# Attention keys and queries projected with the weights stationary and rotated block by block, in one fused attention and mLSTM layer

## The reference

```python
h = rms_norm(x, pre_norm_g[l])
proj = jnp.einsum('bsd,dc->bsc', h, w_in[l])
aq, ak, av, az, mq, mk, mv, mo, mz, mi, mf = split_columns(proj)
ya = moba_attention(partial_rope(att_heads(aq), pos), partial_rope(att_heads(ak), pos), att_heads(av))

def partial_rope(x, pos):            # ROT_DIM = 16 of the 64 columns of a head
    x1 = x[..., :half]
    x2 = x[..., half:ROT_DIM]
    return jnp.concatenate([x1 * cos - x2 * sin, x2 * cos + x1 * sin, x[..., ROT_DIM:]], axis=-1)
```

## Time and profile before

| what | value |
|---|---|
| runs | 323.36 us median (323.27 to 323.56) |
| the profiled execution | 323.28 us, its span 321.5 us |
| PE busy | 313.4 us, 97%, 1626 matmuls |
| DVE busy | 223.3 us, 69%, 527 instructions |
| ACT busy | 167.9 us, 52% |
| POOL busy | 88.2 us, 27% |
| granted TensorE clock | 0.998 |

### The profile page before, as it was taken

One profiled execution on the slowest core, in us unless ns is written; L12 is line 12 of the kernel. 1 busy time (PEld: TensorE's weight loads), 2 busy tenths in 40 slices (PEclk: granted clock), 3 DMA queues, 4 the chain that ended last, 5 costly groups with the idle time before them and its releaser, 6 DMA issues.

```text
span 321.5 us, 5021 instructions
## 1 busy us (share of the span) xinstructions
PE 313.4 (97%) x1626; PEld 260.5 (81%) x1626; DVE 223.3 (69%) x527; ACT 167.9 (52%) x336; POOL 88.2 (27%) x112
## 2 busy tenths in 40 slices
PE   7999999999999999999999999999999999999993
PEld 5887887878888888888888888778888888888882
DVE  2444999758998479976897557775577676865534
ACT  3538852697345434664257442374655976443201
POOL 8001003206350222002220015592621895001000
PEclk9999999999999999999999999999999999999999
DMA  7931553943735491144723332210120264310111
GB/s 234 294 84 50 152 154 92 167 133 93 129 76 143 133 166 39 31 135 139 137 65 98 100 86 80 65 66 34 44 88 2 100 207 153 134 65 2 65 65 65
DMA packets 27016, 33.50 MB, mean 104 GB/s; under 512 B 3768, under 2 KB 15328, under 8 KB 26992
## 3 DMA queue, kind: packets, MB, share of 16 engines
q1 hardware_dynamic: 25712, 30.38, 31.7%
q0 software_dynamic: 1120, 2.68, 6.3%
q10 hardware_dynamic: 160, 0.14, 0.1%
HBM read 31.06 MB, written 2.13 MB: 103 GB/s over the span
## 4 chain that ended last, share of the span: by engine, by line
PE 82%; DVE 9%; issue 5%; ACT 2%; DVEq 0%; POOLq 0%; POOL 0%; ACTq 0%
PE bank L1437 20%; PE bank L1439 20%; PE bank L1438 20%; PE bank L1484 4%; PE bank L1777 3%; PE bank L1721 3%; PE bank L1742 3%; DVE w_lo L980 2%; PE bank L1563 2%; PE bank L1465 1%; DVE farena L1091 1%; PE bank L1671 1%; ACT w_hi L731 1%; DVE rarena L987 1%; PE bank L1732 1%
## 5 line engine op out<-in xcount | busy, mean ns | idle before, releaser
L1437 PE MATMUL bank<-w_hi,xT_hi 128*128 128x512 f32 (+1 forms) x244 | 98.3, 403 | 0.0
L1439 PE MATMUL bank<-w_hi,xT_lo 128*128 128x512 f32 (+1 forms) x244 | 94.9, 389 | 0.0
L1438 PE MATMUL bank<-w_lo,xT_hi 128*128 128x512 f32 (+1 forms) x244 | 94.3, 387 | 0.0
L731 ACT ACTIVATE w_hi<-w_raw 128x512 fp32r<-128x512 f32 x72 | 43.9, 625 | 55.2 <-PE bank L1439 53.1
L1439 PEld LDWEIGHTS bank<-w_hi,xT_lo 128*128 128x128 f32 x244 | 45.8, 188 | 9.8
L1437 PEld LDWEIGHTS bank<-w_hi,xT_hi 128*128 128x128 f32 x244 | 45.9, 188 | 8.0 <-issue 0.4
L1438 PEld LDWEIGHTS bank<-w_lo,xT_hi 128*128 128x128 f32 x244 | 46.0, 189 | 7.6
L980 DVE TENSOR_TENSOR w_lo<-w_raw,w_hi 128x512 fp32r<-128x512 f32 x64 | 45.0, 718 | 4.8 <-ACT w_hi L731 4.5
L908 ACT ACTIVATE rarena<-bank 128x512 fp32r<-128x512 f32 (+3 forms) x32 | 13.9, 436 | 22.5 <-PE bank L1777 22.5
L1437 PE MATMUL bank<-xT_hi,w_hi 128*128 128x512 f32 x64 | 25.6, 400 | 0.0
L1439 PE MATMUL bank<-xT_hi,w_lo 128*128 128x512 f32 x64 | 25.1, 392 | 0.0
(11 more groups left out here) (206 smaller groups left out, 595.8 us busy)
## 6 DMA issues: line engine op xcount, KB each, us to landing
w_raw<-in_w_in SPq DMA_DIRECT2D x72, 256.0 KB, 2.8
w_raw<-in_w_out SPq DMA_DIRECT2D x16, 256.0 KB, 2.6
gy<-in_x SPq DMA_DIRECT2D x4, 512.0 KB, 5.4
out_y<-gy SPq DMA_DIRECT2D x7, 256.0 KB, 2.0
farena<-in_x SPq DMA_DIRECT2D x4, 256.0 KB, 4.7
farena<-in_x SPq DMA_DIRECT2D x2, 512.0 KB, 6.6
farena<-g_rows POOLq DMA_DIRECT2D x4, 256.0 KB, 4.0
farena<-g_rows POOLq DMA_DIRECT2D x4, 192.0 KB, 5.8
```

The source lines that it names most:

```text
L731: a.activation(w_hi[:, n % RING, :], w_raw[:, n % RAW, :], ACT.Copy).then_inc(w_hi_done, 1)
L1437: pe.matmul(o, hi, m_hi, start=start, stop=False)
L1438: pe.matmul(o, hi, m_lo, start=False, stop=False)
L1439: return pe.matmul(o, lo, m_hi, start=False, stop=stop)
```

## The change

- Keys and queries are projected with the weights stationary (`by_block`): the block m of 128 columns (two heads) lies on the partitions, the tokens lie along the row, and nothing has to be turned. `turn_k`, `turn_q`, `k_copy`, `q_copy` and the old `rope` go.
- The rotation works on whole blocks: `plain` = block x cosine table and `crossed` = block with its rows exchanged by a shuffle of 32 partitions (both on DVE, from PSUM, `kq_rows`), then on POOL (`kq_sum`) `crossed` x sine table and the sum of both. The high and low parts are then taken from SBUF (`k_high`, `k_low`, `q_high`, `q_low`).
- The tables are full: 128 partitions by 512 tokens, with 1 and 0 where nothing rotates. Four DMAs of POOL load the short table in the first microseconds, PE turns it once (`rope_rows`, in bank 6), ACT copies four parts of it (`rope_part`), and POOL multiplies both tables by the norm of x (`tables`). The sine table lies in `gains` until the queries are done, so the second gain row is loaded later.
- The groups' order becomes az, ak, aq, av. Values are copied by ACT to `stage` and split from there.
- Gate rows: the input gate's bias goes to ACT, the negation of the maxima to ACT, the last difference (`rows[4]`) to POOL. `gate_cols` uses bank 7; `emt` is taken in loop 18, behind both silus of head 0.
- On POOL the sums stand between the decay rows, the square roots and the masks of heads 2 and 3.

The diff, cut to its core:

```diff
-for _h, _c in enumerate((AZ, AK, AV, AQ)):
+for _h, _c in enumerate((AZ, AK, AQ, AV)):
...
-                if n == S_AV + 4:
-                    sp.wait_ge(az_gained, NT)
+                if n == S_MO:
+                    sp.wait_ge(kq_ready, 2 * NT)
                     sp.dma_start(gains[:], mlstm_g.to_broadcast([P, AW])).then_inc(gain_in, 16)
...
+            for q in range(4):
+                g.dma_start(rope_cols[:, :, q, 0:ROT],
+                            rope[:, ROT * (q % 2):ROT * (q % 2 + 1)].rearrange("(t p) c -> p t c", p=P)).then_inc(rope_in, 16)
...
+            g.wait_ge(gmax_done, 1)
+            g.tensor_tensor(rows[4], rows[1], rows[2], ALU.subtract).then_inc(grows_done, 1)
...
-            for h in range(1, MH):
-                decay_rows(h)
-                head_rsqrt(2 * h - 2)
-                decay_mask(h)
-                head_rsqrt(2 * h - 1)
+            def tables():
+                g.wait_ge(rope_rows_done, 4)
+                g.wait_ge(rbc_done, 1)
+                g.tensor_tensor(cos_t, cos_raw, rbc[:], ALU.mult).then_inc(tables_done, 1)
+                g.tensor_tensor(sin_t, sin_raw, rbc[:], ALU.mult).then_inc(tables_done, 1)
+            def kq_sum(w, m):
+                n = NT * w + m
+                g.wait_ge(tables_done, 2)
+                g.wait_ge(kq_crossed, n + 1)
+                g.tensor_tensor(crossed[w][:, m, :], crossed[w][:, m, :], sin_t, ALU.mult).then_inc(kq_scaled, 1)
+                g.wait_ge(kq_scaled, n + 1)
+                g.wait_ge(kq_plain, n + 1)
+                g.tensor_tensor(plain[w][:, m, :], plain[w][:, m, :], crossed[w][:, m, :], ALU.add).then_inc(kq_ready, 1)
+            decay_rows(1)
+            head_rsqrt(0)
+            decay_mask(1)
+            head_rsqrt(1)
+            tables()
+            for w in range(2):
+                kq_sum(w, 0)
+                kq_sum(w, 1)
+                decay_rows(w + 2)
+                head_rsqrt(2 * w + 2)
+                kq_sum(w, 2)
+                head_rsqrt(2 * w + 3)
+                kq_sum(w, 3)
+                decay_mask(w + 2)
...
+            a.activation(rows[6], gate_rows[0:16, :], ACT.Identity, bias=bcol[:, 0:1]).then_inc(igate_done, 1)
...
-                if b == S_QK + 7:
+                if b == ST_AT[0]:
                     a.wait_ge(aT_done, 1)
...
+            def k_high(m):
+                a.wait_ge(kq_ready, m + 1)
+                a.activation(kT_hi[:, m, :], plain[0][:, m, :], ACT.Copy).then_inc(kt_hi, 1)
...
+            def kq_rows(w, m):
+                projected(v, ("ak", "aq")[w], m)
+                v.wait_ge(tables_done, 2)
+                if w:
+                    v.wait_ge(kq_ready, m + 1)
+                    v.wait_ge(kt_lo, m + 1)
+                v.tensor_tensor(plain[w][:, m, :], bank[m][:], cos_t, ALU.mult).then_inc(kq_plain, 1)
+                v.stream_shuffle(crossed[w][:, m, :], bank[m][:],
+                                 [i // ROT * ROT + (i + HALF) % ROT for i in range(32)]).then_inc(kq_crossed, 1)
...
+                    for m in (2 * c, 2 * c + 1):
+                        if b == S_AQ - 3 + c:
+                            kq_rows(0, m)
+                        if b == S_AV - 3 + c:
+                            kq_rows(1, m)
+                        if b == S_MZ + 3 + c:
+                            v_low(m)
...
+            def by_block(n, k, free):
+                low_done(pe, n)
+                for m in range(4):
+                    if k == 0:
+                        free(m)
+                    mm = product(bank[m][:], *w_part(n, slice(m * P, (m + 1) * P)), xT_hi[:, k, :], xT_lo[:, k, :],
+                                 k == 0, k == NK - 1)
```

More of the change, by code:

```diff
@@ L113 @@
 EVENTS = {}
-PRIORITY = ("mz", "mz_late", "z", "slot", "z_part", "part", "part_q", "q_T", "q_out", "ya_half", "ya", "ya_sq", "ya_ms",
+PRIORITY = ("mz", "mz_late", "z", "slot", "z_part", "part", "part_q", "q_out", "ya_half", "ya", "ya_sq", "ya_ms",
             "ya_gate", "y_sq", "y", "y_q_sq", "y_q", "y_fin", "y_end", "cut", "turn")
@@ L312, in build @@
         bcol = pcol[0:16, R_BIAS:R_END]
-        keys = queries = stage
+        plain, crossed = (stage, gate), (gate, stage)
+        cos_t, sin_t = f_part(F_COS, SEQ), gains[:]
+        cos_raw, sin_raw = stage[:, 3, :], stage[:, 2, :]
+        rope_cols = silu_az[:, 3, :].rearrange("p (t q d) -> p t q d", t=NT, q=4)
         post = stage[:, 0:2].rearrange("p a c -> p (a c)")
@@ L426, in build @@
         ym_gated = sem("ym_gated")
-        k_raw = sem("k_raw")
-        k_roped = sem("k_roped")
-        kt_ps = sem("kt_ps")
+        rope_clear = sem("rope_clear")
+        rope_ps = sem("rope_ps")
+        rope_set = sem("rope_set")
+        rope_rows_done = sem("rope_rows_done")
+        tables_done = sem("tables_done")
+        kq_plain = sem("kq_plain")
+        kq_crossed = sem("kq_crossed")
+        kq_scaled = sem("kq_scaled")
+        kq_ready = sem("kq_ready")
+        v_raw = sem("v_raw")
         kt_hi = sem("kt_hi")
@@ L783, in decays, with rope_part @@
                     .then_inc(decay_done, 1)
+            def rope_part(q):
+                a.wait_ge(rope_ps, 1)
+                a.wait_ge(rope_set, 2)
+                to = 2 * ROT * (q // 2 * 2)
+                a.activation((cos_raw, sin_raw)[q % 2][to:to + 2 * ROT, :], bank[6][2 * ROT * q:2 * ROT * (q + 1), :],
+                             ACT.Copy).then_inc(rope_rows_done, 1)
             def conv_silu(n):
@@ L832, in _ @@
                 if b == S_MZ + 1:
-                    for i in range(NT):
-                        q_copy(i)
+                    for t in range(NT):
+                        v_copy(t)
                 cut(b + AHEAD)
@@ L1559, in head_values @@
                     pe.wait_ge(num_done, NT * h + t - 1)
+                else:
+                    pe.wait_ge(emt_done, 1)
                 o = bank[7 - t % 2]
@@ L1579, in _ @@
             rx_rows()
+            rope_rows()
             mv_slot(NK - 1)
@@ L1598, in qk_slot @@
                 mm.then_inc(w_used, 1)
-            def turn_k(t):
-                pe.wait_ge(k_roped, t + 1)
-                if t < 2:
-                    pe.wait_ge(u_done, 5 + t)
-                else:
-                    pe.wait_ge(kt_lo, t - 1)
-                for k in range(4):
-                    mm = pe.transpose(bank[4 + t % 2][:, k * P:(k + 1) * P], keys[:, t, k * P:(k + 1) * P], ident[:])
-                mm.then_inc(kt_ps, 1)
-            def turn_q(i):
-                pe.wait_ge(q_roped, i + 1)
-                if i < 2:
-                    pe.wait_ge(u_done, 7 + i)
-                else:
-                    pe.wait_ge(qt_lo, i - 1)
-                for k in range(4):
-                    mm = pe.transpose(bank[4 + i % 2][:, k * P:(k + 1) * P], queries[:, i, k * P:(k + 1) * P], ident[:])
-                mm.then_inc(qt_ps, 1)
+            def by_block(n, k, free):
[5 more added lines that the diff above has]
+                                 k == 0, k == NK - 1)
+                    if k == NK - 1 and m < 3:
+                        mm.then_inc(proj_ps, 1)
+                mm.then_inc(w_used, 1)
             def mz_slot(b):
-                by_slot(b, b - S_MZ, NK, x_part, lambda t: pe.wait_ge(q_raw, t + 1))
+                by_slot(b, b - S_MZ, NK, x_part, lambda t: pe.wait_ge(v_raw, t + 1))
             for b in range(S_QK, LAST_SLOT):
@@ L1718, in pair_scores @@
                     for q, half in enumerate(rows_of):
-                        lhs = qT[half, 2 * i + (step == 2), cols]
+                        lhs = (q_lo if step == 2 else q_hi)[half, h // 2, t * P:(t + 1) * P]
                         keys_of = kT_lo if step == 1 else kT_hi
```

205 lines of the change are left out of this document (79 added, 126 removed).

## The result

| what | before | after |
|---|---|---|
| runs | 323.35 us median (323.27 to 323.85) | 330.47 us median (330.25 to 333.15) |
| ratio | | 1.0242 (1.0207 to 1.0277) |
| profiled execution, span | 323.28, 321.5 us | 330.62, 328.9 us |

What follows compares the result with a forecast made beforehand. PE, busy for 97% of the span, was taken as the bound, with DVE's small reserves deciding. -3.5 + 0.44 - 0.89 + 0.95 + 3.4 + 0.75 + 3.2 = +4.35 us on 323.28 gave 327.6 us, range 320.3 to 331.0.

Steps and rivals of the forecast that it cites:

- Transposes, -3.5 + 0.44: On PE, 32 transposes of roped keys and queries go, -3.5 us; one group for the table rows comes, +0.44.
- The gate steps, -0.89: PE's stall at 70.25 to 71.37 goes: three gate operations leave DVE, emt moves behind both silus; 0.89 us gained.
- The tables, +0.95: Loops 28 to 30: POOL's two table products hold DVE, weighted ends near 104.05, PE waits 0.95 us.
- Keys, +3.4, and queries, +3.2: Loops 33 to 40 and 45 to 52: new DVE work and POOL's holds delay qk_low; PE waits 3.4 and 3.2 us.
- the same terms: The keys' chain of DVE steps reused for the queries, from 150.16 to 179.1, wanted at 175.89.
- weighted(2,0), +0.75: One step after the keys' wait: ACT's late silu puts DVE's weighted at 144.55, PE ready at 143.8; 0.75 us.
- the first steps of attention: Value copies go through stage and v_low stands where ropes of the same length stood; no cost counted.
- What the profile would show: Waits of 3.4, 3.2 at qk_low, 0.95 at weighted; convolution additions over 0.9 us, low cut over 0.8, POOL some 110.
- Rival 1: POOL's work finds gaps, DVE loses nothing, only PE's work counts: -3.95, 319.3 us; chance 0.18.
- the locks: POOL's operations hold about 1.25 us each; DVE operations with two SBUF inputs wait, those with a PSUM input do not.
- Rival 2: POOL's hold on DVE costs half of what was counted, 4.15 of 8.3 us of stalls: 323.5 us; chance 0.13.
- Rival 3: The shuffle takes 1.2 us, 2.2 us more in each stretch: 332.0 us; chance 0.05, including late table rows.

Runs made afterwards that it cites:

- 2: The changed kernel without DVE's eight shuffles (rotation left out, POOL's 16 operations keep their length): 327.31 us.
- 4: The changed kernel with the rotation's products and sums on DVE in place of POOL, k_high and k_low two loops later: 322.32 us, ratio 0.9965.
- the first of 5: The changed kernel with POOL's two table products put ahead of the decay rows of head 1: 331.85 us.
- 10: The kernel before, with only DVE's copy of the gate columns one loop earlier (14 instead of 15): 322.75 us, ratio 0.9982.
- 9: Changed kernel with sums on DVE, tables behind weighted(1,1), values one loop earlier, v_copy awaiting its own block, emt put back between ACT's two silus: 320.51 us.
- 11: The kernel before with extra DVE subtractions ahead of qk_low(5) and qk_low(7): six and six 333.31 us, three and nine 331.21 us.

## Why the prediction was right and wrong

- **Transposes, -3.5 + 0.44.** Right: the page has 28 PE instructions less, no turning in slots 37 to 40 and 59 to 62, and the group for the table rows costs 0.43 us (33.84 to 34.27). In this trace everything from the first slots on is another 0.5 us late:
```profile
33.84 0.60 PE L1546 MATMUL bank<-ident,rx 128*128 128x128 f32 x4
34.27 0.60 PE L1554 MATMUL bank<-ident,silu_az 128*128 128x128 f32 x4
```

and the `rx` group before:

```profile
33.30 0.60 PE L1527 MATMUL bank<-ident,rx 128*128 128x128 f32 x4
```

That is no cost of the change: the `rx` group starts at 33.26 to 33.28 in the traces of 2, 4 and the first of 5, which load the tables in the same way, and at 33.56 in that of 10, which loads none.
- **The gate steps, -0.89.** The size was right (PE's gap at 70 is gone), the reason wrong in half. emt's new place is not needed (9); the earlier copy of the gate columns and the shorter gate steps are what counts (10).
- **The tables, +0.95.** Measured 1.07. The way was not quite the one told: `hsc` waits 1.25 us and the norm's two steps, with one SBUF input each, take 1.53 where I let two cuts be held:

```profile
99.31 1.31 POOL L661 TENSOR_TENSOR farena<-stage,rbc 128x512 f32<-128x512 f32 x1
99.38 1.25 DVE L1201 TENSOR_TENSOR hsc<-vr,iden 128x2 f32<-128x2 f32 x1
...
100.55 1.31 POOL L662 TENSOR_TENSOR gains<-stage,rbc 128x512 f32<-128x512 f32 x1
...
100.67 1.53 DVE L1203 TENSOR_SCALAR gy<-num,mva,hsc 128x128 f32<-128x128 f32 x2
...
104.15 0.41 PE L1456 MATMUL bank<-rarena 128*128 128x384 f32 x1 [0.91 <-DVE farena L1154]
```

- **Keys, +3.4, and queries, +3.2.** Measured 3.39 and 3.41. For the queries "the same terms" were added 0.3 us too low (from 169.8 they give 175.7 and 179.4, so 3.5). That the sums hit is in part luck, since they rest on errors that cancel: the convolution's first step was taken to run freely beside POOL and was held for 1.0 us (1.50 against 0.55), while its additions lost 0.9 and 1.1 us and not 1.9 and 2.35. And the terms do not simply add (2).
- **weighted(2,0), +0.75.** Not seen in the kernel after, since PE itself was slow there; it comes out, as 0.77, where the clock stays up (2).
- **What was missing, first:** the clock. I priced a wait of PE at its length. Behind the first one another 1.5 us went (1.85 to 2.0 by the differences between runs), and in two of six runs, by their mean clock, probably a second time. This is the step that failed: a wait put on PE was taken to go on the time at its own length, with no term for what comes after it.
- **What was missing, second:** the first steps of attention. "Value copies go from PSUM through stage ... v_low stands where ropes of the same length stood" let them cost nothing: a term set to zero, the second step that failed. Two `v_low` took 2.38 and 2.06 us beside POOL's cuts, and q_low and the norm were held as well:

```profile
213.00 2.55 POOL L644 TENSOR_TENSOR w_lo<-w_raw,w_hi 128x512 fp32r<-128x512 f32 x2
213.08 1.24 DVE L1201 TENSOR_TENSOR hsc<-vr,iden 128x2 f32<-128x2 f32 x1
214.35 1.53 DVE L1203 TENSOR_SCALAR gy<-num,mva,hsc 128x128 f32<-128x128 f32 x2
...
219.93 0.96 PE L1738 MATMUL bank<-rarena 64*128 64x512 f32 x6 [0.62 <-DVE mx L1329]
...
221.97 0.47 PE L1456 MATMUL bank<-w_hi,xT_hi 128*128 128x512 f32 x1 [0.48 <-DVE gy L1290]
```

From the last matmul ahead of these waits (218.93) to the product at 221.97 it is 3.04 us, where the same instructions took 1.67 before (213.01 to 214.68): +1.4.

Together: -3.1 - 0.9 + 1.1 + 3.4 + 3.4 + 1.5 + 1.4 = +6.8 us, of +7.3 in the profiled execution. The last 0.5 us is the late start of this execution, shown under the transposes. What the profile would show came in most points (the waits' names and sizes, 0.935 us for the additions); two signs missed: the low cut took 0.746 us on average and not over 0.8, and POOL was busy for 121.5 us and not some 110.

Rival 1 (POOL costs DVE nothing, 319.3 us) was wrong of this kernel, but named about what the locks cost in all: with the sums cut short the time was 321.7 us, of which 2.3 us are still the waits at 102 and at the first attention steps (an estimate from both: 319.4), and with the sums on DVE and the rest moved, 320.0. Rival 2 (half the price of the locks) is refuted by the two waits, which came in full. Rival 3 is refuted by the shuffle's 0.74 us (0.63 from start to start).

## What to carry to other kernels

An operation of 128x512 with two inputs in SBUF, given to POOL beside a busy DVE, freed no time on DVE here: 16 of them held it for 9.7 us, and doing them itself took it 9.1 us (238.1 against 229.0 with the sums cut short; 16 x 0.6 would be 9.6). Look at which of DVE's instructions lie beside them; those that read PSUM ran at their own pace beside POOL, those with their tensors in SBUF were held. And price a wait of TensorE of 3.4 us or more at its length plus 1.5 to 2 us for the slower matmuls behind it; six of the seven such waits in these traces had them. From this, two waits of 1.7 us should be cheaper than one of 3.4; no run here tried that.

## What the runs showed of the hardware

- POOL's two-input operations held a single-input operation of DVE as well, where it read SBUF: TENSOR_SCALAR on 128x512, 1.50 us for 0.55. Even a two-input one on 128x2 took 1.25 us for 0.15. Multiplications and shuffles from PSUM kept their 0.68 and 0.74 us. The Trainium skill ("GPSIMD Engine Reference", "1. Specifications") names both kinds, two SBUF inputs and the mode with two ports; by "VectorE: DVE Perf Modes" ("Mode 2×_2P") the latter reads one SBUF tensor through both read ports. The trace agrees in that both kinds were held; that the TENSOR_SCALAR ran in this mode no row shows. In the prediction I had used only the first half of that rule.
- TensorE behind a pause: from the first matmul on (141.36) or five matmuls later (183.65 in 11), for some 2 to 4 us (once 5.7, in the first trace of 5), matmuls of 512 columns at 0.43 us. The Trainium skill ("TensorE: Matmul & The Clock Gate", Part 1) says that the clock has two levels, full and half; 0.43 against 0.227 us agrees. Two waits of the same kernel, 3.39 and 3.41 us long, differed: slow clock behind the first and full clock behind the second. And its executions had mean clocks of 0.989 or 0.979.
